# Hybrid decoder trunk on one core: attention units with their own step orders, weight splits moved within them, K weights scaled one pair ahead on GpSimd

## The chip, the cores and the metric

One core of one Trainium2 chip runs the whole program in one launch. The metric is the device time of that core in microseconds. The core has TensorE (PE for matmuls, PEld for its weight loads), VectorE (DVE), ScalarE (ACT), GpSimd (POOL) and SyncE (SP, which issues most DMAs here).

## The reference

Two layers over a residual stream of 1024 tokens by 1024 channels: a recurrent layer (RG-LRU) with a SwiGLU block, then a forgetting-attention layer with a SwiGLU block. The change lies in the attention layer:

```python
p = rmsnorm(h, norm_kv) @ w_kvf          # K, V and 16 forget logits
k, v, c = K heads, V heads, cumsum(log_sigmoid(f + b_forget))
q = rmsnorm(h, norm_mix[1]) @ w_q        # 16 heads of 64
for blk in range(8):                     # 128 queries each, causal
    s = q_blk @ k[:q1].T / 8 + c[q] - c[k]
    p = softmax(where(mask, s, -inf))
    out_blk = p @ v[:q1]
h = h + concat(out) @ w_o
```

All of it is float32 to the accuracy of a split: each matmul operand is written as high + low (both fp32r), and a product takes three matmuls.

## The kernel before, in words

Every engine has its own instruction stream, written out by hand and synchronised by counting semaphores; within an engine the order is fixed. Activations lie transposed in SBUF, 8 tiles of 128 channels by 1024 tokens (`xh`, `xl`). A weight piece of 128 x 1024 is loaded by SyncE into `raw`; ScalarE writes its high half `wh` (`split_hi`, L914), VectorE the low half `wl` (`split_lo`, L1256). `raw`, `wh` and `wl` have four slots; attention uses slots 0 and 1 in turn. In attention GpSimd first multiplies each `raw` piece by the norm's gain (`gain_piece`, L542).

Attention goes over 8 **pairs** of heads. Beside the scores of pair i, TensorE projects K and Q of pair i+1: 32 steps `p` of three 512-column matmuls each, eight for a half (1024 tokens are two halves of 512). After every eighth `p` VectorE must drain the one PSUM bank of the projections (`project_half`, L1588 for K, L1590 for Q) before the ninth may start. A pair has 8 **units** (2 heads x 4 ranges of 256 queries, ranges in the order 3, 0, 2, 1, so the unit's size differs). The steps of a unit are tokens of a string in `UNIT_STEPS`, and PE, ACT and DVE all walk through the same string:

- `S0`, `S1`: scores of the *next* unit, first and second 128 queries (L758 to L761). DVE takes the row maximum (`nmax`, L1667), ACT the exponential into `probs` (L1163).
- `T0`..`T3`: transposes of `probs` (L780), 256 keys each; ACT copies the high half `pth` (L1193), DVE the low half `ptl` (L1673). The first transpose of a unit waits for both exponentials.
- `V0`..`V3`: values times probabilities (L793), each waits for its `ptl`.
- `O`: the previous unit's output is added by ACT (`o_low`) and DVE into `resid`.
- `p`: a projection step (L746). `X`, `Y`: transposes of V (L823) and their two halves into `vs` (ACT L1183, DVE L1660 and L1661). `R`: the transposed row sums.

Ahead of unit 0 stands `A S0 S1 B` (called unit -1): `A` and `B` project V of this pair, 24 matmuls each. Between pairs ACT makes the halves of K (`kh`, L1130 and L1135) and of Q (L1147, L1148), DVE their low halves (L1596, L1602). `S1` of unit -1 shares its PSUM with `A` and waits until DVE has drained that (`kv_tmp`, L1655). `S1` of unit 0 uses the PSUM tile in which V was transposed, and waits until `vs` is written.

Pair 0 is written out, pairs 1 to 6 are a loop of three rounds of two, and pair 7 is written out without `p` steps. After it the output projection starts (`wo_tile`, L857) from `ohl`, the halves of the attention output (ACT L1152, DVE L1640), and its weight pieces, split by the same two routines.

Of the kernel before, what the change touches and what calls it, by code (L numbers as in the profile page):

```python
# [19 lines left out]
class Turns:  # L20
# [27 lines left out]


RANGE_ORDER = [3, 0, 2, 1]  # L50
UNIT_STEPS = {
# [4 lines left out]
}  # L56
PAIR_START = "A S0 S1 B"


WEIGHTS_AT = {(-1, "S1"): "K", (1, "S1"): "Q", (5, "S1"): "nextV"}  # L60


def pair_steps(with_p):

    steps = [(-1, s) for s in PAIR_START.split()]
    units = 2 * len(RANGE_ORDER)
    for u in range(units):
        for s in UNIT_STEPS[RANGE_ORDER[u % len(RANGE_ORDER)]].split():
            if u == 0 and s == "O" or u == units - 1 and s[0] == "S":
                continue  # L70
            steps.append((u, s))
            if (u, s) == (0, "T0"):
                steps += [(u, "X"), (u, "Y")]
            if (u, s) == (units - 1, "T1"):
                steps.append((u, "R"))
    steps.append((units, "O"))
    return [x for x in steps if x[1] != "p" or with_p]


def hawk_fox_yoco(nc, x, norm_mix, norm_ffn, w_ffn_in, w_ffn_out, w_rec_in, conv_w, conv_b,  # L80
# [11 lines left out]
    S, D = x.shape[1], x.shape[2]  # L92
# [7 lines left out]
    PAIRS = HEADS * HD // P  # L100
# [12 lines left out]
    pieces = Turns(4)  # L113
# [27 lines left out]
    STAT = {"start": 0, "recE": 1, "ffn0E": 2, "attE": 3, "ffn1E": 4}  # L141
    LRU_STEPS, FORGET_STEPS = 16, 10
    T_PAIR = RANGES * (RANGES + 1)

    with ExitStack() as life:
        def sb(name, shape, dt, at=life):
# [88 lines left out]
        v_filled = sem("v_filled")  # L235
# [35 lines left out]
        w_gained = sem("w_gained")  # L271
# [57 lines left out]
        GAIN = {"K": V_KV, "V": V_KV, "Q": V_MIX + KT}  # L329
# [184 lines left out]
        @block.gpsimd  # L514
        def _(pool):
            pool.memset(ident[:, :], 0.0)
            pool.memset(ones[:, :], 1.0)
            pool.memset(identb[:, :], 0.0)
            pool.memset(maskb[:, :], 0.0)
            pool.memset(negsel[:, :], 0.0).then_inc(const_zero, 1)  # L520
            pool.wait_ge(const_zero, 1)
            for m in (ident, identb):
                pool.affine_select(out=m[:, :], in_=m[:, :], compare_op=ALU.not_equal, fill=1.0, base=0,
                                   pattern=[[-1, P]], channel_multiplier=1)
            pool.affine_select(out=maskb[:, :], in_=maskb[:, :], compare_op=ALU.is_ge, fill=NEG, base=0,
                               pattern=[[-1, P]], channel_multiplier=1)
            pool.affine_select(out=negsel[:, :], in_=negsel[:, :], compare_op=ALU.not_equal, fill=-1.0, base=0,
                               pattern=[[-1, HEADS]], channel_multiplier=1).then_inc(const_zero, 1)
            pool.wait_ge(const_zero, 2)
            for n, base in enumerate((-32, -64, -96)):  # L530
                last = pool.affine_select(out=negsel[:, :], in_=negsel[:, :], compare_op=ALU.not_equal, fill=-1.0,
                                          base=base, pattern=[[-1, HEADS]], channel_multiplier=1)
                last.then_inc(const_ready if n == 2 else const_zero, 1)
                pool.wait_ge(const_ready if n == 2 else const_zero, 1 if n == 2 else 3 + n)

            def gain_piece(use, gain, n=P):

                slot, count = use
                pool.wait_ge(loaded[slot], count * 16)
                w = raw[slot][:, :].rearrange("p (k n) -> p k n", k=KT)[:, :, 0:n]  # L540
                g = vec[:, gain:gain + KT].unsqueeze(2).broadcast_to([P, KT, n])
                pool.tensor_tensor(w, w, g, ALU.mult).then_inc(w_gained, 1)  # L542

            def select(i):
                for j in range(2):
                    other = slice((1 - j) * HD, (2 - j) * HD)
                    pool.tensor_copy(q2[other, j, :], negsel[other, bass.ds(i * 2 + j, 1)].broadcast_to([HD, S])
                                     ).then_inc(sel_ready, 1)
                    pool.wait_ge(sel_ready, i * 2 + (j + 1))

            def scale_o(i):

                pool.wait_ge(rinv_loaded, i * 32 + 32)
                pool.wait_ge(o_added, i * UNITS + UNITS)
                o = resid[:, i, :] if isinstance(i, int) else resid[:, bass.ds(i, 1), :]
                r = rinv[:, :] if isinstance(i, int) else rinv[:, :].unsqueeze(1)
                pool.tensor_tensor(o, o, r, ALU.mult).then_inc(o_scaled, 1)

            def pool_pair(i, uses, with_p=True):
                pool.wait_ge(ql_ready, i * 2 + 2)  # L560
                if with_p:
                    gain_piece(uses["K"], GAIN["K"])
                    gain_piece(uses["Q"], GAIN["Q"])
                if not (isinstance(i, int) and i == 0):
                    scale_o(i - 1)
                if with_p:
                    pool.wait_ge(o_added, i * UNITS + 4)
                    gain_piece(uses["nextV"], GAIN["V"])
                    pool.wait_ge(s_filled, i * (2 * QB) + 2 * QB)
                    pool.wait_ge(w_gained, GAINED["V"](i + 1))  # L570
                    select(i + 1)

            gain_piece(pieces.use("forget", 0), V_KV, HEADS)
            for j, kind in enumerate("KQV"):
                gain_piece(pieces.use("attA", j), GAIN[kind])
            pool.wait_ge(c_ready, 1)
            pool.wait_ge(w_gained, GAINED["V"](0))
            select(0)
            pool_pair(0, att_uses(0))
            with pool.Fori(0, (PAIRS - 2) // 2) as it:  # L580
                for d in range(2):
                    pool_pair(it * 2 + (d + 1), att_uses(None, it, d))
            pool_pair(PAIRS - 1, att_uses(PAIRS - 1, None, 1), with_p=False)
            scale_o(PAIRS - 1)

# [316 lines left out]
        def _(act):  # L902
# [272 lines left out]
            def pair(i, uses, with_p=True):  # L1175
                high_q(i, f_before(i))
                for u, step in pair_steps(False):
                    m = int(step[1]) if len(step) > 1 else 0
# [15 lines left out]
                    elif step == "O":  # L1194
# [1 line left out]
                        if u >= 3:  # L1196
                            act.wait_ge(o_added, i * UNITS + (u - 2))
                        act.activation(o_low[(u - 1) % 2][:, :], o_ps[HD:P, :], ACT.Copy).then_inc(o_low_ready, 1)
                    if with_p and (u, step) in WEIGHTS_AT:
                        kind = WEIGHTS_AT[u, step]  # L1200
                        split_hi(uses[kind], att_free(kind, i),
                                 scaled=GAINED[kind[-1]](i + 1))
                    if with_p and (u, step) == (UNITS - 1, "T1"):
                        high_k(i + 1, f_before(i + 1) - 2)
                    if (u, step) == (UNITS - 1, "R"):
# [13 lines left out]
                for d in range(2):  # L1219
                    pair(it * 2 + (d + 1), att_uses(None, it, d))  # L1220
            pair(PAIRS - 1, att_uses(PAIRS - 1, None, 1), with_p=False)
            for m in range(2):
                split_hi(pieces.use("attE", m), (v_filled, 2 * PAIRS))
            act.wait_ge(o_added, PAIRS * UNITS)
            for k in range(PAIRS // 2, PAIRS):
                high_o(k)
# [22 lines left out]
        def _(dve):  # L1249
# [168 lines left out]
            steps = [2]  # L1418
# [224 lines left out]
            def pair(i, uses, with_p=True):  # L1643
# [3 lines left out]
                p = 0  # L1647
                for u, step in pair_steps(with_p):
                    m = int(step[1]) if len(step) > 1 else 0
# [43 lines left out]
                    elif step == "p":  # L1693
                        p += 1
                        if p % KT == 0:
                            q = p // KT - 1
                            project_half(q // 2, q % 2, kq_count(i + 1, q // 2, q % 2))
                    if with_p and (u, step) in WEIGHTS_AT:
                        split_lo(uses[WEIGHTS_AT[u, step]])

            pair(0, att_uses(0))
            with dve.Fori(0, (PAIRS - 2) // 2) as it:
# [52 lines left out]
```

## Time and profile before

| | |
|---|---|
| median of 3 runs | 2624.01 us (2622.91 to 2625.97) |
| the profiled execution | 2628.85 us, of which the span is 2627.0 us |
| PE busy | 2487.4 us (95%) |
| PEld, DVE, ACT, POOL busy | 77%, 48%, 30%, 3% |
| mean granted TensorE clock | 0.977 |
| attention pairs | from 1172.9 to 1744.8 us of the span |

TensorE is busy nearly all the time, so the places that count are the few in which it waits. The trace gives for every instruction its start and length and, where an engine sat idle before it, for how long and what ended that. A matmul's end is modelled: matmuls overlap, the next may start before the last one's end. Start to start is the safer measure.

### The profile page before, as it was taken

How to read it: one execution, taken by the hardware profiler on the slowest of the kernel's cores; microseconds unless marked ns; L12 is line 12 of the kernel's file. 1: busy time of each engine (PE TensorE's matmuls, PEld its weight loads, DVE VectorE, ACT ScalarE, POOL GpSimd, SP SyncE). 2: the span in 40 equal slices, each digit the busy share in tenths (PEclk: the TensorE clock that was granted, in tenths of full speed). 3: DMA queues.
4: the chain of work that ended last, by engine and by line, in shares of the span. 5: the costliest groups of instructions: out<-in, count | busy, mean ns of one | idle time of the engine just before them, and what ended most of it. 6: DMA issues, size and time to landing. Idle time of an engine off the chain costs nothing.

```text
span 2627.0 us, 28888 instructions
## 1 busy us (share of the span) xinstructions
PE 2487.4 (95%) x11449; PEld 2026.3 (77%) x11449; DVE 1262.3 (48%) x1257; ACT 782.6 (30%) x1045; POOL 85.9 (3%) x65
## 2 busy tenths in 40 slices
PE   7999889999999999989998989969999999999998
PEld 5888768888888888767777777757788888888887
DVE  6567664444444444465555555553444444444443
ACT  4443541111111111245454545542211111111112
POOL 0000000000000000010111111000000000000000
PEclk9999999999999999999999999989999999999998
DMA  3111011111111111111010110021111111111101
GB/s 113 57 56 48 24 33 55 50 48 48 48 48 48 48 48 49 56 48 33 25 33 24 32 30 26 25 89 48 48 49 49 49 49 51 50 48 48 48 24 64
DMA packets 164159, 122.65 MB, mean 47 GB/s; under 512 B 5136, under 2 KB 144640, under 8 KB 164096
## 3 DMA queue, kind: packets, MB, share of 16 engines
q1 hardware_dynamic: 162352, 117.52, 14.7%
q10 hardware_dynamic: 1744, 4.32, 0.6%
q8 instruction: 36, 0.59, 0.1%
q14 instruction: 27, 0.22, 0.0%
HBM read 113.37 MB, written 8.45 MB: 46 GB/s over the span
## 4 chain that ended last, share of the span: by engine, by line
PE 84%; DVE 6%; issue 5%; ACT 4%; DMA 1%; ACTq 0%; DVEq 0%; SPq 0%
PE ps L602 66%; PE ps L746 6%; PE ps L857 3%; PE ps L640 2%; PE ps L793 2%; PE ps L780 1%; DVE ptl L1673 1%; ACT pth L1193 1%; DVE nmax L1667 1%; PE ps L758 1%; PE ps L761 1%; PE ps L636 1%; ACT kh L1130 1%; ACT probs L1163 1%; ACT wh L914 0%
## 5 line engine op out<-in xcount | busy, mean ns | idle before, releaser
L602 PE MATMUL ps<-xh,wh 128*128 128x512 f32 x1680 | 519.5, 390 | 3.9 <-DVE wl L1256 2.5
L602 PE MATMUL ps<-xl,wh 128*128 128x512 f32 x1680 | 518.0, 390 | 0.0
L602 PE MATMUL ps<-xh,wl 128*128 128x512 f32 x1680 | 517.9, 389 | 0.0
L602 PEld LDWEIGHTS ps<-xh,wh 128*128 128x128 f32 x1680 | 315.9, 188 | 72.4 <-issue 7.0
L1293 DVE TENSOR_TENSOR tmp<-ps,rstd 128x1024 f32<-128x1024 f32 x96 | 117.3, 1224 | 528.0 <-PE ps L602 527.9
L602 PEld LDWEIGHTS ps<-xl,wh 128*128 128x128 f32 x1680 | 315.9, 188 | 65.8
L602 PEld LDWEIGHTS ps<-xh,wl 128*128 128x128 f32 x1680 | 315.8, 188 | 65.7
L1299 DVE TENSOR_TENSOR resid<-ps,resid 128x1024 f32<-128x1024 f32 x216 | 261.6, 1222 | 211.1 <-PE ps L602 211.1
L1256 DVE TENSOR_TENSOR wl<-raw,wh 128x1024 fp32r<-128x1024 f32 x193 | 236.9, 1232 | 218.4 <-ACT wh L914 218.3
L914 ACT ACTIVATE wh<-raw 128x1024 fp32r<-128x1024 f32 x193 | 201.3, 1049 | 417.8 <-PE ps L602 349.7
L602 PE MATMUL ps<-hh,wh 128*128 128x512 f32 x704 | 221.7, 396 | 9.8 <-DVE hl L1525 9.8
L602 PE MATMUL ps<-hl,wh 128*128 128x512 f32 x704 | 218.7, 392 | 0.0
L602 PE MATMUL ps<-hh,wl 128*128 128x512 f32 x704 | 218.3, 391 | 0.0
L1072 ACT ACTIVATE hh<-tmp 128x1024 fp32r<-128x1024 f32 x44 | 46.7, 1061 | 493.0 <-DVE tmp L1521 493.0
L746 PE MATMUL ps<-xh,wh 128*128 128x512 f32 x384 | 162.8, 424 | 16.6 <-DVE kv_tmp L1588 6.0
L602 PEld LDWEIGHTS ps<-hh,wh 128*128 128x128 f32 x704 | 132.9, 190 | 40.0 <-DVE hl L1525 10.7
L602 PEld LDWEIGHTS ps<-hl,wh 128*128 128x128 f32 x704 | 133.3, 189 | 28.2
L602 PEld LDWEIGHTS ps<-hh,wl 128*128 128x128 f32 x704 | 133.3, 189 | 28.2
L746 PE MATMUL ps<-xh,wl 128*128 128x512 f32 x384 | 153.4, 400 | 0.0
L746 PE MATMUL ps<-xl,wh 128*128 128x512 f32 x384 | 153.0, 398 | 0.0
L1068 ACT ACTIVATE tmp<-tmp 128x1024 f32<-128x1024 f32 x44 | 46.6, 1060 | 332.2 <-DVE tmp L1293 332.2
L1673 DVE TENSOR_TENSOR ptl<-ps,pth 128x512 fp32r<-128x512 f32 (+1 forms) x160 | 98.0, 634 | 88.2 <-ACT pth L1193 86.9
(184 smaller groups left out, 2796.1 us busy)
## 6 DMA issues: line engine op xcount, KB each, us to landing
raw<-in_w_ffn_in SPq DMA_DIRECT2D x88, 512.0 KB, 3.8
raw<-in_w_ffn_out SPq DMA_DIRECT2D x44, 512.0 KB, 3.3
raw<-in_w_rec_in SPq DMA_DIRECT2D x16, 512.0 KB, 5.2
raw<-in_w_kvf SPq DMA_DIRECT2D x16, 512.0 KB, 3.9
xin<-in_x SPq DMA_DIRECT2D x8, 512.0 KB, 6.9
raw<-in_w_rec_out SPq DMA_DIRECT2D x8, 512.0 KB, 4.0
raw<-in_w_q SPq DMA_DIRECT2D x8, 512.0 KB, 3.9
spill<-resid SPq DMA_DIRECT2D x8, 512.0 KB, 2.6
```

Source lines behind the costliest of these rows:

```text
L602: last = pe.matmul(acc[:, h], w, v[:, h], start=(k == 0 and p == 0), stop=(k == len(terms) - 1 and p == 2))
L640: last = pe.matmul(ps[3][:, h], ones[:, :], sq(seg, k)[:, h], start=(k == 0), stop=(k == KT - 1))
L746: last = pe.matmul(acc, w, v[:, k, h], start=(k == 0 and p == 0), stop=(k == KT - 1 and p == 2))
L793: last = pe.matmul(o_ps[:, q0 * P:2 * P], v, pt[t % 2][:, col:col + n], start=(kb == 0 and pt is pth), stop=(kb == 2 * r + 1 and pt is ptl))
L857: last = pe.matmul(acc[:, h], w, ohl[:, k, v, h], start=(k == 0 and p == 0), stop=(k == KT - 1 and p == 2))
L914: act.activation(wh[slot][:, :], raw[slot][:, :], ACT.Copy).then_inc(hi_ready[slot], 1)
L1068: act.activation(tmp[t][:, :], tmp[t][:, :], ACT.Silu).then_inc(silu_ready, 1)
L1072: act.activation(hh[:, t, :], tmp[2 + t][:, :], ACT.Copy).then_inc(hh_ready, 1)
L1256: dve.tensor_tensor(wl[slot][:, :], raw[slot][:, :], wh[slot][:, :].bitcast(F32), ALU.subtract).then_inc(lo_ready[slot], 1)
L1293: dve.tensor_tensor(dst, ps[slot][:, :], rstd[:, :], ALU.mult).then_inc(drained[slot], 1)
L1299: dve.tensor_tensor(resid[:, m, :], ps[slot][:, :], resid[:, m, :], ALU.add).then_inc(drained[slot], 1)
L1673: dve.tensor_tensor(ptl[t % 2][:, 0:width], t_ps[t % 2][:, 0:width], pth[t % 2][:, 0:width].bitcast(F32), ALU.subtract).then_inc(ptl_ready, 1)
```

## The change

Each of the 8 units now has its own string; `X`, `Y` and `R` stand in the strings, and the scores `S0`, `S1` of units 0, 2, 4 and 6 are spread between later steps. ACT's high split and DVE's low split of a weight piece now have places of their own (`HI_AT`, `LO_AT`). In pair 7 the first two output-weight pieces are split inside the pair (`OUT_AT`) and no longer behind it. GpSimd multiplies K of pair i+2 by its gain at the end of its work for pair i (`next_k`) where it did K of pair i+1 at the start; its loop is one round shorter for that, with the last round written out.

```diff
-UNIT_STEPS = {
-    3: "O T0 T1 S0 S1 p V0 T2 p V1 T3 p V2 p V3 p",
-    0: "O T0 S0 S1 p V0 p p",
-    2: "O T0 T1 S0 S1 p V0 T2 p V1 p V2 p",
-    1: "O T0 T1 S0 S1 p V0 p V1 p p",
-}
+UNIT_STEPS = [
+    "T0 X Y T1 p p p V0 T2 p V1 T3 S0 p V2 S1 V3",
+    "O T0 S0 S1 p V0 p p",
+    "O T0 T1 S0 p V0 T2 S1 p V1 p V2 p",
+    "O T0 T1 S0 S1 p V0 p V1 p p",
+    "O T0 T1 p p V0 T2 p V1 T3 S0 p V2 S1 p V3",
+    "O T0 S0 S1 p V0 p p",
+    "O T0 T1 S0 p V0 T2 S1 p V1 p V2 p",
+    "O T0 T1 R p p V0 p V1 p",
+]
...
-WEIGHTS_AT = {(-1, "S1"): "K", (1, "S1"): "Q", (5, "S1"): "nextV"}
+HI_AT = {(-1, "A"): "K", (1, "T0"): "Q", (5, "T0"): "nextV"}
+LO_AT = {(-1, "S1"): "K", (1, "V0"): "Q", (5, "V0"): "nextV"}
...
+    OUT_AT = {(1, "V0"): 0, (5, "V0"): 1}
...
-            def pool_pair(i, uses, with_p=True):
+            def pool_pair(i, uses, next_k=None, with_p=True):
                 pool.wait_ge(ql_ready, i * 2 + 2)
                 if with_p:
-                    gain_piece(uses["K"], GAIN["K"])
                     gain_piece(uses["Q"], GAIN["Q"])
...
                     gain_piece(uses["nextV"], GAIN["V"])
+                    if next_k is not None:
+                        gain_piece(next_k, GAIN["K"])
                     pool.wait_ge(s_filled, i * (2 * QB) + 2 * QB)
...
                         split_hi(uses[kind], att_free(kind, i),
                                  scaled=GAINED[kind[-1]](i + 1))
+                    if not with_p and (u, step) in OUT_AT:
+                        split_hi(pieces.use("attE", OUT_AT[u, step]), (v_filled, 2 * PAIRS))
...
             pair(PAIRS - 1, att_uses(PAIRS - 1, None, 1), with_p=False)
-            for m in range(2):
-                split_hi(pieces.use("attE", m), (v_filled, 2 * PAIRS))
             act.wait_ge(o_added, PAIRS * UNITS)
...
-            for m in range(2):
-                split_lo(pieces.use("attE", m))
```

In the order of TensorE's instructions, unit 0 of the first pair read so before, from its `T0` on (`kv_tmp` is V, `q2`, `qs`, `kl`, `kh` are the scores' operands, the last three rows a step `p`):

```order
L780 MATMUL ps2<-ident,probs0 128x128 x4
L823 MATMUL ps1<-ident,kv_tmp 128x128 x8
L780 MATMUL ps2<-ident,probs0 128x128 x4
L758 MATMUL ps0<-kl,q2 128x128
L760 MATMUL ps0<-maskb,identb 128x128
L761 MATMUL ps0<-kh,qs 128x128
L758 MATMUL ps1<-kl,q2 128x256
L760 MATMUL ps1<-maskb,identb 128x128
L761 MATMUL ps1<-kh,qs 128x256
L746 MATMUL ps3<-xh,wh1 128x512
L746 MATMUL ps3<-xl,wh1 128x512
L746 MATMUL ps3<-xh,wl1 128x512
```

Now, from the same `T0` (all lines of the program stand 5 lower from here on):

```order
L785 MATMUL ps2<-ident,probs0 128x128 x4
L828 MATMUL ps1<-ident,kv_tmp 128x128 x8
L785 MATMUL ps2<-ident,probs0 128x128 x4
L751 MATMUL ps3<-xh,wh1 128x512
L751 MATMUL ps3<-xl,wh1 128x512
L751 MATMUL ps3<-xh,wl1 128x512
L751 MATMUL ps3<-xh,wh1 128x512
L751 MATMUL ps3<-xl,wh1 128x512
L751 MATMUL ps3<-xh,wl1 128x512
L751 MATMUL ps3<-xh,wh1 128x512
L751 MATMUL ps3<-xl,wh1 128x512
L751 MATMUL ps3<-xh,wl1 128x512
```

The six matmuls of `S0` and `S1` are gone from behind `T1`, and three steps `p` stand there. The scores now come at the unit's end. Before, the last steps up to the next unit's `T0` (`probs1`) were:

```order
L746 MATMUL ps3<-xh,wh1 128x512
L746 MATMUL ps3<-xl,wh1 128x512
L746 MATMUL ps3<-xh,wl1 128x512
L793 MATMUL ps3<-pth1,vs 128x256
L793 MATMUL ps3<-ptl1,vs 128x256
L793 MATMUL ps3<-pth1,vs 128x128
L793 MATMUL ps3<-ptl1,vs 128x128
L746 MATMUL ps3<-xh,wh1 128x512
L746 MATMUL ps3<-xl,wh1 128x512
L746 MATMUL ps3<-xh,wl1 128x512
L780 MATMUL ps2<-ident,probs1 128x128 x3
```

Now, from `V2` on, they are:

```order
L798 MATMUL ps3<-pth0,vs 128x256
L798 MATMUL ps3<-ptl0,vs 128x256
L798 MATMUL ps3<-pth0,vs 128x256
L798 MATMUL ps3<-ptl0,vs 128x256
L763 MATMUL ps1<-kl,q2 128x256
L765 MATMUL ps1<-maskb,identb 128x128
L766 MATMUL ps1<-kh,qs 128x256
L798 MATMUL ps3<-pth1,vs 128x256
L798 MATMUL ps3<-ptl1,vs 128x256
L798 MATMUL ps3<-pth1,vs 128x128
L798 MATMUL ps3<-ptl1,vs 128x128
L785 MATMUL ps2<-ident,probs1 128x128 x3
```

`S1` (into `ps1`) now ends only four short matmuls ahead of the `T0` that needs its exponential, and no `p` stands between. On ScalarE, from unit 1's `O` to unit 2's `T0` and `T1`, stood before:

```order
L1198 ACTIVATE o_low<-ps 64x256
L1193 ACTIVATE pth<-ps 128x384
L1163 ACTIVATE probs,rsum<-ps,nmax 128x640
L1163 ACTIVATE probs,rsum<-ps,nmax 128x768
L914 ACTIVATE wh<-raw 128x1024
L1198 ACTIVATE o_low<-ps 64x256
L1193 ACTIVATE pth<-ps 128x512 x2
```

and now:

```order
L1203 ACTIVATE o_low<-ps 64x256
L1198 ACTIVATE pth<-ps 128x384
L919 ACTIVATE wh<-raw 128x1024
L1168 ACTIVATE probs,rsum<-ps,nmax 128x640
L1168 ACTIVATE probs,rsum<-ps,nmax 128x768
L1203 ACTIVATE o_low<-ps 64x256
L1198 ACTIVATE pth<-ps 128x512 x2
```

The split of Q's weights (`wh`) moves from behind the two exponentials to ahead of them. On VectorE the low split stays between the two maxima and the drain of K.

## Rows read from the trace of the kernel before

**Rows 1.** Stretches: us, busy us (instructions) of PE, PEld, DVE, ACT, POOL; granted clock; DMA.

```profile
1244.00:1315.80 71.80, 66.10 (x371) 53.75 (x370) 41.30 (x60) 38.16 (x74) 10.08 (x6) 0.98 0.11 30
1315.80:1386.20 70.40, 64.49 (x371) 52.35 (x370) 41.19 (x60) 38.17 (x74) 10.09 (x6) 1.00 0.11 31
1683.90:1744.80 60.90, 46.92 (x271) 38.91 (x270) 35.22 (x54) 31.99 (x67) 2.38 (x1) 0.91 0.03 9
...
1262.90:1266.30 3.40, 3.40 (x14) 3.11 (x14) 0.75 (x3) 1.02 (x4) 0.00 (x0) 0.50 0.02 7
```

**Rows 2.** TensorE's waits, pair 2: who waits for whom, us, times, longest.

```profile
PE ps L758 <- DVE vs L1661: 1.8, 1, 1.8
PE ps L793 <- DVE ptl L1673: 1.6, 4, 0.5
PE ps L758 <- DVE kv_tmp L1655: 0.9, 1, 0.9
PE ps L746 <- DVE kv_tmp L1588: 0.6, 1, 0.6
PE ps L746 <- DVE q_tmp L1590: 0.6, 1, 0.6
```

**Rows 3.** Timeline of unit 0, pair 2: start, length, engine, line, [idle before].

```profile
1329.83 0.60 PE L780 MATMUL ps<-ident,probs 128*128 128x128 f32 x4
...
1331.10 0.69 DVE L1673 TENSOR_TENSOR ptl<-ps,pth 128x512 fp32r<-128x512 f32 x1 [0.30 <-ACT pth L1193]
...
1333.70 0.68 DVE L1661 TENSOR_TENSOR vs<-ps,vs 128x512 fp32r<-128x512 f32 x1
...
1334.44 0.38 PE L758 MATMUL ps<-kl,q 128*128 128x256 f32 x1 [1.81 <-DVE vs L1661]
...
1334.90 0.63 DVE L1667 TENSOR_REDUCE nmax<-ps 128x1 f32<-128x128 f32 x2
...
1335.58 0.47 ACT L1163 ACTIVATE probs<-ps,nmax 128x256 f32<-128x256 f32 x1
...
1339.86 0.28 PE L793 MATMUL ps<-pth,vs 128*128 128x256 f32 x1
...
1340.26 0.45 PE L746 MATMUL ps<-xh,wh 128*128 128x512 f32 x1
...
1341.01 0.49 PE L780 MATMUL ps<-ident,probs 128*128 128x128 f32 x3
```

**Rows 4.** Timeline, units 1 and 2 of pair 2.

```profile
1343.46 0.80 ACT L1163 ACTIVATE probs<-ps,nmax 128x640 f32<-128x640 f32 x1 [1.36 <-DVE nmax L1667]
...
1345.22 1.05 ACT L914 ACTIVATE wh<-raw 128x1024 fp32r<-128x1024 f32 x1
...
1346.30 1.23 DVE L1256 TENSOR_TENSOR wl<-raw,wh 128x1024 fp32r<-128x1024 f32 x1 [2.01 <-ACT wh L914]
...
1348.18 0.50 PE L746 MATMUL ps<-xh,wh 128*128 128x512 f32 x1 [0.61 <-DVE kv_tmp L1588]
```

**Rows 5.** Timeline from pair 1's last unit to pair 2's second scores.

```profile
1310.59 0.93 PE L780 MATMUL ps<-ident,probs 128*128 128x128 f32 x7
...
1312.17 2.12 ACT L1130 ACTIVATE kh<-kv_tmp 64x1024 fp32r<-64x1024 f32 x2
...
1323.20 0.50 PE L758 MATMUL ps<-kl,q 128*128 128x512 f32 x1 [0.88 <-DVE kv_tmp L1655]
```

**Rows 6.** Timeline of GpSimd and VectorE at the start of pair 2.

```profile
1326.27 2.40 POOL L557 TENSOR_TENSOR resid<-resid,rinv 128x1024 f32 x1
...
1328.01 1.75 DVE L1256 TENSOR_TENSOR wl<-raw,wh 128x1024 fp32r<-128x1024 f32 x1 [2.22 <-ACT wh L914]
```

**Rows 7.** Timeline between the last pair and the output projection.

```profile
1750.12 6.79 DVE L1640 TENSOR_TENSOR ohl<-resid,ohl 128x1024 fp32r<-128x1024 f32 x4
...
1756.84 2.35 DVE L1256 TENSOR_TENSOR wl<-raw,wh 128x1024 fp32r<-128x1024 f32 x2
...
1758.16 2.05 PE L857 MATMUL ps<-ohl,wh 128*128 128x512 f32 x4 [12.43 <-DVE wl L1256]
```

More of the change, by code:

```diff
@@ L50 @@
 RANGE_ORDER = [3, 0, 2, 1]
-UNIT_STEPS = {
[4 rows of a table removed]
-}
+UNIT_STEPS = [
[8 rows of a table added]
+]
 PAIR_START = "A S0 S1 B"
-WEIGHTS_AT = {(-1, "S1"): "K", (1, "S1"): "Q", (5, "S1"): "nextV"}
+HI_AT = {(-1, "A"): "K", (1, "T0"): "Q", (5, "T0"): "nextV"}
+LO_AT = {(-1, "S1"): "K", (1, "V0"): "Q", (5, "V0"): "nextV"}
 def pair_steps(with_p):
     steps = [(-1, s) for s in PAIR_START.split()]
[L66 to L76, printed above, removed]
+    for u, unit in enumerate(UNIT_STEPS):
+        steps += [(u, s) for s in unit.split()]
+    steps.append((len(UNIT_STEPS), "O"))
     return [x for x in steps if x[1] != "p" or with_p]
@@ L568, in pool_pair @@
                     gain_piece(uses["nextV"], GAIN["V"])
+                    if next_k is not None:
+                        gain_piece(next_k, GAIN["K"])
                     pool.wait_ge(s_filled, i * (2 * QB) + 2 * QB)
-                    pool.wait_ge(w_gained, GAINED["V"](i + 1))
+                    pool.wait_ge(w_gained, GAINED["V"](i + 1) + (next_k is not None))
                     select(i + 1)
@@ L578, in _ @@
             select(0)
-            pool_pair(0, att_uses(0))
-            with pool.Fori(0, (PAIRS - 2) // 2) as it:
+            gain_piece(att_uses(0)["K"], GAIN["K"])
+            pool.wait_ge(w_gained, GAINED["K"](1))
+            pool_pair(0, att_uses(0), att_uses(None, 0, 0)["K"])
+            with pool.Fori(0, (PAIRS - 2) // 2 - 1) as it:
                 for d in range(2):
-                    pool_pair(it * 2 + (d + 1), att_uses(None, it, d))
+                    nxt = att_uses(None, it, 1) if d == 0 else att_uses(None, it + 1, 0)
+                    pool_pair(it * 2 + (d + 1), att_uses(None, it, d), nxt["K"])
+            last = (PAIRS - 2) // 2 - 1
+            pool_pair(PAIRS - 3, att_uses(None, last, 0), att_uses(None, last, 1)["K"])
+            pool_pair(PAIRS - 2, att_uses(None, last, 1))
             pool_pair(PAIRS - 1, att_uses(PAIRS - 1, None, 1), with_p=False)
@@ L1198, in pair @@
                         act.activation(o_low[(u - 1) % 2][:, :], o_ps[HD:P, :], ACT.Copy).then_inc(o_low_ready, 1)
-                    if with_p and (u, step) in WEIGHTS_AT:
-                        kind = WEIGHTS_AT[u, step]
+                    if with_p and (u, step) in HI_AT:
+                        kind = HI_AT[u, step]
                         split_hi(uses[kind], att_free(kind, i),
                                  scaled=GAINED[kind[-1]](i + 1))
+                    if not with_p and (u, step) in OUT_AT:
+                        split_hi(pieces.use("attE", OUT_AT[u, step]), (v_filled, 2 * PAIRS))
                     if with_p and (u, step) == (UNITS - 1, "T1"):
@@ L1697, in pair @@
                             project_half(q // 2, q % 2, kq_count(i + 1, q // 2, q % 2))
-                    if with_p and (u, step) in WEIGHTS_AT:
-                        split_lo(uses[WEIGHTS_AT[u, step]])
+                    if with_p and (u, step) in LO_AT:
+                        split_lo(uses[LO_AT[u, step]])
+                    if not with_p and (u, step) in OUT_AT:
+                        split_lo(pieces.use("attE", OUT_AT[u, step]))
             pair(0, att_uses(0))
```

## The prediction

> **What bounds the kernel now.** I read the views in this order. The page's sums say that TensorE is busy for 95% of the span, so only its waits count, and the change touches only attention. The view by stretches gives the pairs: pair 2 takes 70.4 us at full clock, pair 1 takes 71.8 us with one dip to half clock (1.2 of 2.4 GHz) of 3.4 us, and the last pair, which has no projections, 60.9 us [rows 1]. The view of waits, narrowed to pair 2, lists what TensorE stands for: 1.8 us until V's halves are written, 1.6 us in four waits for `ptl`, 0.9 us until VectorE has drained `A`, twice 0.6 us until it has drained a projection's half [rows 2]. Another 0.4 us goes before `X`, and those six sums are the whole idle time of the pair (70.40 - 64.49 = 5.9 us [rows 1]). A listed wait is shorter than what it costs: a `p` of three matmuls takes 0.75 us from start to start, 0.25 each, while one matmul lasts 0.45 in its row [rows 3], so each modelled end lies 0.2 us late. A wait costs its row and 0.2 us more.
>
> **The change, part by part.** The strings of the units only reorder: each pair has the same 32 `p`, the same scores, transposes and values. So I take away the waits that get cover and add those that lose it.
>
> Unit 0. From its `T0` to unit 1's `T0` go 11.18 us (1329.83 to 1341.01) [rows 3], the largest wait among them: `S1` stands until `vs` is written at 1334.38. Now three `p` of 0.7 to 0.8 us stand there, 2.2 us after `T1`, and what follows, `V0`, needs the same `vs`: it comes about 0.1 us after the third `p`. That takes away 1.8 + 0.2 - 0.1 = 1.9 us. But the exponential of `S1` now decides when unit 1's `T0` may start. Before, `S1` began at 1334.44; its maximum was out at 1335.53, the exponential ran from 1335.58 for 0.47, and some 0.1 us is left for reading out the row sum: 1.7 us in all. `S1` itself holds TensorE for 0.46 us, and `V3` for 0.40 (1339.86 to 1340.26) [rows 3]. So `T0` waits 1.7 - 0.46 - 0.40 = 0.8 to 0.9 us. Unit 0 nets 1.0 us. Before, five steps lay between and hid it.
>
> Units 1 and 5. ScalarE stands idle for 1.36 us ahead of its exponentials for unit 2, and the split of Q's weights, 1.05 us, came behind them at 1345.22; VectorE waited 2.01 us for it, its low split ran until 1347.53, and only then was K's half drained, which TensorE waited for until 1348.18 [rows 4]. With the high split behind `T0`'s `pth`, it fits into the 1.36 us with 0.3 to spare. The low split can start when the second maximum is out, about 0.9 us before 1345.22 (the second exponential runs in between), ends near 1345.5, and the drain waits for the eighth `p` alone. `O` and `ptl`, queued behind the drain, come earlier by about 1.2 us too. If that cover were gone, the split would delay both exponentials, and with them unit 2's `T0`, by at most 1.05 us per split. Units 5 and 6 repeat this with the next V's weights.
>
> Units 2 and 6. The two drain waits (0.6 each) and three of the four `ptl` waits (1.2 of the 1.6 us; the fourth is in unit 7) lie here [rows 2]. From a `T` to its `V` go 2.0 us (1329.83 until 1331.79 and the semaphore) [rows 3]. In the new string `V2` stands behind `T2` by `S1`, `p`, `V1`, `p`, some 2.7 us; ScalarE has one exponential of 0.6 us to do in between, which just fits. So all five go: 1.2 + 1.2 + 5 x 0.2 = 3.4 us.
>
> Unit 4. `S0` and `S1` move as in unit 0, but one `p` stands between `V3` and `T0`: 1.7 - 0.46 - 0.40 - 0.7 leaves 0.1 to 0.2 us of a new wait. Nothing was lost here before.
>
> Unit 7. One `p` more stands ahead of `V0`, which hides the fourth `ptl` wait (0.4 + 0.2). I count it at nothing. Behind this unit runs a chain that does not care for TensorE: ScalarE's four K halves start at 1312.17, right after `pth` of the `T0` of 1310.59, of which the first two take 2.12 us; then the other two, `o_low`, VectorE's add, its four low halves and the drain of `A`, until `S1` of unit -1 starts at 1323.20 [rows 5]. That is 12.6 us from `T0`; TensorE, freed, just waits there 0.6 us longer than now (0.88 listed).
>
> GpSimd. K's gain leaves the start of the pair and comes behind V's in unit 4. At the start it is not on the path: K's first `p` stands 10 us later. Here the row shows contention: the low split of K takes 1.75 us at 1328.01 while GpSimd's scaling runs until 1328.67 [rows 6], and 1.23 us alone [rows 4]. With GpSimd done 1.9 us earlier and the split moved up to about 1326, either finds its place before `B` ends at 1330. In unit 4 VectorE does only `ptl`, maxima and `o_low` additions, each with one operand in PSUM. The Trainium skill, page "SBUF — State Buffer", section "Who interferes with whom", says that a VectorE instruction with two SBUF inputs contends with a GpSimd instruction that reads SBUF, and one with at most one SBUF input doesn't; by that rule the moved gain costs nothing in unit 4, and the 1.75 us agree. `select`, queued behind it, has until the next pair. SyncE's loads are released by the same low splits, in the same order, K's some 2 us earlier: nothing.
>
> So a pair nets 1.9 - 0.9 + 3.4 - 0.2 = 4.2 us, and seven pairs 29 us. The waits at the loop's back edge (between pairs 2 and 3, and 4 and 5) are untouched.
>
> The clock. Pairs 1, 4, 5 and 6 each have a dip of 3.4 us that begins at the `vs` wait, such as the one at 1262.9; it costs 71.8 - 70.4 = 1.4 us [rows 1]. Pair 2 has the same wait and no dip. The new order still has 1.5, 0.4 and 0.9 us of waiting within some 20 us. I take half of the four dips away: 3 us; ends 0 and 6. The Trainium skill, "TensorE: Matmul & The Clock Gate", section "What's actually happening", says that the default is the throttled state and that activity releases it. By that alone all four dips would go, and the sum would be 3 us lower; the rows of pair 2 show that the wait is not enough to cause one.
>
> Pair 7 has no `p` to cover anything. Unit 0 gains 0.9 us (the `vs` wait, less what it puts before `V3` and `T0`). In units 2 and 6 `V0` comes sooner in the string, while ScalarE and VectorE must do the output weights' halves (1.05 and 1.23 us [rows 4]) ahead of `o_low` and `pth`: `V0` 0.7 us later, and `S1`'s exponential, now behind `T2`'s `ptl`, 1 us later: 1.7 us each. Unit 4 loses 0.7. Sum +3 us; ends 0 and 6.
>
> The end. Behind pair 7 TensorE waits 12.43 us for the first output weight's low half, which VectorE makes only after four low halves of `ohl` (from 1750.12 for 6.79 us, 1.7 each) [rows 7]. With the weights ready, the first matmuls can start after the first of the four, near 1751.9, but are then fed at 1.7 and later 1.2 us per tile of six matmuls, which take 1.36 at full clock; seven tiles are fed until 1759.4, and the other nine follow: 1759.4 + 10 x 1.36 = 1773, against 1781.6 before. The first tiles run at half clock, 2.7 us each; I take 6 us of the 8.4 (ends 4 and 8.5).
>
> The sum: -29 - 3 + 3 - 6 = -35 us. The profiled execution took 2628.85 us (span 2627.0), which gives 2594; against the median of 2624.0, 4.8 us lower, 2589.
>
> **The rivals.** First, late scores: `S0`, `S1` behind `T3` put their maxima and exponentials into the queues just before `T0`'s `pth`; if each such join in units 0, 2, 4 and 6 costs 0.7 us more than worked out, a pair nets 1.5 us, and the time is 2624 - 10 - 6 = 2608. For it speaks that the exponential in unit 2 fits only just; against it the 2.0 us from `T` to `V`, which hold. Second, more than forecast: all dips vanish (3 us more), the end gives 8.5, pair 7 loses nothing: 2624 - 29 - 6 - 8.5 = 2580, and with a start chain that gives back unit 7's 0.6 per pair, 2576. Third, on the other side, the clock: the waits now gather at the pair's start and at unit 1's `T0`. If TensorE fell to 1.2 GHz there for long, at 1.4 us lost per 3.4 us of dip, then 40 us, that is 97 us of dips or 14 us in each pair, make it slower: 2630 and above. Pair 2 with 5.9 us of idle time and no dip speaks against it. Fourth, the covers bring nothing, as the chain of ScalarE and VectorE through a whole pair decides, and only pair 7 and the end count: 2624 + 3 - 6 = 2621. Against it: they are busy for 38 and 41 of 70 us [rows 1].
>
> **How the numbers follow.** As worked out, 2589 (its own range 2579 to 2600): 0.60. More: 0.08. Late scores, 2600 to 2618: 0.20. No change, within 0.2% (5.2 us, about what a measurement of this kernel can tell): 0.05. Slower: 0.07. The range of 2573 to 2607 leaves out the last two, some 0.06 of the late scores and 0.01 below. Faster 0.88, same 0.05, slower 0.07.
>
> **What would show it.** In the profile after: the wait on `vs` gone from `S1` and under 0.3 us at `V0`; no wait of a `p` on L1588 or L1590's drain; one wait of 0.8 us at unit 1's `T0` on `probs`; the wait of unit -1's `S1` near 1.5 us; pairs of 66 us; the first output matmul some 6 us after the last value. It would be wrong if pairs stay above 69 us, if `T0` waits over 2 us, or if the granted clock in attention falls below the 0.98 of pair 1.

## The result and the profile after

The changed kernel takes **2587.64 us** (median of 4 runs, 2585.63 to 2593.28), the kernel before, run beside it, 2624.28 us. The ratio is 0.9864, with a 95% interval of 0.9846 to 0.9881. Its profiled execution took 2588.48 us. The page of the profile after:

```profile
span 2586.7 us, 28872 instructions
PE 2471.5 (96%) x11449; PEld 2021.3 (78%) x11449; DVE 1266.3 (49%) x1257; ACT 787.3 (30%) x1045; POOL 85.9 (3%) x65
```

The same stretches as in [rows 1], in the kernel after: pairs 1, 2, 3 and 7.

```profile
1236.90:1302.90 66.00, 63.38 (x371) 52.62 (x370) 41.87 (x60) 38.61 (x74) 10.09 (x6) 1.00 0.11 33
1302.90:1369.20 66.30, 63.50 (x371) 52.70 (x370) 42.25 (x60) 38.74 (x74) 10.07 (x6) 1.00 0.12 33
1369.20:1441.60 72.40, 66.69 (x371) 54.66 (x370) 40.83 (x60) 38.75 (x74) 10.05 (x6) 0.95 0.10 30
1645.50:1710.00 64.50, 46.10 (x271) 38.39 (x270) 37.41 (x56) 35.02 (x70) 2.38 (x1) 0.92 0.03 9
```

Pair 2 has gone from 70.4 to 66.3 us, the last pair from 60.9 to 64.5. Pair 1, which had a dip to half clock before, has none now. In pair 2, TensorE's list of waits, against [rows 2]:

```profile
PE ps L763 <- DVE kv_tmp L1660: 1.5, 1, 1.5
PE ps L785 <- ACT probs L1168: 0.7, 1, 0.7
PE ps L828 <- DVE kv_tmp L1660: 0.4, 1, 0.4
PE ps L798 <- DVE vs L1666: 0.2, 1, 0.2
```

Together 2.8 us, which is 66.30 - 63.50, the pair's whole idle time; it was 5.9 us. The two waits for a projection's drain and the four for `ptl` are gone. The wait for `vs` has shrunk to 0.2 us and stands at `V0`, the one ahead of `S1` of unit -1 has grown from 0.9 to 1.5 us, and one of 0.7 us at unit 1's `T0` is new. This is unit 0 on the timeline after, against [rows 3]:

```profile
1322.34 0.38 PE L798 MATMUL ps<-pth,vs 128*128 128x256 f32 x1 [0.17 <-DVE vs L1666]
...
1326.32 0.28 PE L763 MATMUL ps<-kl,q 128*128 128x256 f32 x1
...
1326.88 0.42 DVE L1672 TENSOR_REDUCE nmax<-ps 128x1 f32<-128x256 f32 x1 [0.48 <-PE ps L766]
...
1327.34 0.47 ACT L1168 ACTIVATE probs<-ps,nmax 128x256 f32<-128x256 f32 x1 [0.45 <-DVE nmax L1672]
...
1327.96 0.55 PE L785 MATMUL ps<-ident,probs 128*128 128x128 f32 x3 [0.71 <-ACT probs L1168]
```

`S1` begins at 1326.32 and unit 1's `T0` at 1327.96: 1.64 us, in which maximum and exponential run one behind the other with nothing beside them on TensorE but `V3`. Next, units 1 and 2 after, against [rows 4]:

```profile
1329.01 1.05 ACT L919 ACTIVATE wh<-raw 128x1024 fp32r<-128x1024 f32 x1
...
1330.47 0.80 ACT L1168 ACTIVATE probs<-ps,nmax 128x640 f32<-128x640 f32 x1 [0.41 <-DVE nmax L1672]
...
1331.22 1.22 DVE L1261 TENSOR_TENSOR wl<-raw,wh 128x1024 fp32r<-128x1024 f32 x1
...
1332.68 0.69 DVE L1593 TENSOR_TENSOR kv_tmp<-ps,rstd 128x512 f32<-128x512 f32 x1 [0.25 <-PE ps L751]
```

ScalarE's idle time ahead of the exponential is 0.41 instead of 1.36 us, with the high split in it. VectorE goes into the low split without a wait, where it stood for 2.01 us, and the drain (`kv_tmp`, last row) now waits for TensorE and not TensorE for it. At the end, against [rows 7]:

```profile
1715.76 11.35 DVE L1645 TENSOR_TENSOR ohl<-resid,ohl 128x1024 fp32r<-128x1024 f32 x8
...
1717.14 2.05 PE L862 MATMUL ps<-ohl,wh 128*128 128x512 f32 x4 [6.58 <-DVE ohl L1645]
...
1720.36 1.59 PE L862 MATMUL ps<-ohl,wh 128*128 128x512 f32 x4 [0.32 <-DVE ohl L1645]
```

TensorE waits 6.58 us for the first `ohl` low half where it waited 12.43 us for the weights.

The balance of the two profiled executions, from the trace (start to start): pairs 0 to 6 took 511.0 us before and 473.4 now (-37.6), pair 7 +3.6, from the last value's first matmul to the 96th of the output 36.5 and 31.1 us (-5.4), what lies ahead of pair 0 -0.9. Together -40.3, the difference of the spans. The last of these is chance: over all traces pair 0 starts between 1170.5 and 1174.9 us.

### The profile page after: what moved, and what is told of

Read it like the earlier page. It is cut to its first block, busy times and chain, and to the rows that moved or that the text cites. A ratio compares the mean times of both kernels' runs of the same rounds, so it can differ in the third digit from the quotient of the medians.

```text
span 2586.7 us, 28872 instructions
## 1 busy us (share of the span) xinstructions
PE 2471.5 (96%) x11449; PEld 2021.3 (78%) x11449; DVE 1266.3 (49%) x1257; ACT 787.3 (30%) x1045; POOL 85.9 (3%) x65
## 4 chain that ended last, share of the span: by engine, by line
PE 90%; DVE 4%; issue 3%; ACT 2%; DMA 0%; ACTq 0%; SPq 0%; DVEq 0%
PE ps L607 67%; PE ps L751 8%; PE ps L862 3%; PE ps L798 3%; PE ps L785 2%; PE ps L645 2%; PE ps L766 1%; PE ps L763 1%; PE ps L641 1%; ACT kh L1135 1%; DVE kl L1601 0%; DVE kv_tmp L1660 0%; DMA xin<-in_x 0%; PE ps L828 0%; DVE wl L1261 0%
## 5 line engine op out<-in xcount | busy, mean ns | idle before, releaser
L607 PEld LDWEIGHTS ps<-xl,wh 128*128 128x128 f32 x1680 | 315.6, 188 | 65.7
```

What stands on the lines that cost most here:

```text
L607: last = pe.matmul(acc[:, h], w, v[:, h], start=(k == 0 and p == 0), stop=(k == len(terms) - 1 and p == 2))
```

## The experiments

All times are medians of 4 to 10 runs (but for the last kernel, one run) beside runs of the kernel before on the same chip (2624.2 to 2625.9 us). "Pair" is the length of pair 2, or of pairs 4 and 6 where pair 2 has a dip of the clock.

**The strings alone.** Splits (those of the output weights too) and gain go back to their old places; the cut shows the two tables.

```diff
-HI_AT = {(-1, "A"): "K", (1, "T0"): "Q", (5, "T0"): "nextV"}
-LO_AT = {(-1, "S1"): "K", (1, "V0"): "Q", (5, "V0"): "nextV"}
+HI_AT = {(-1, "S1"): "K", (1, "S1"): "Q", (5, "S1"): "nextV"}
+LO_AT = {(-1, "S1"): "K", (1, "S1"): "Q", (5, "S1"): "nextV"}
...
```

> The new step strings alone: weight splits at S1 of units -1, 1 and 5 as before, K's gain at the pair's start as before, the output weights' splits behind pair 7. If the strings and the splits each carry a part (my theory): unit 0 keeps its 1.1 us, units 2 and 6 still meet a late drain of the projection bank, since the split lies ahead of it, and keep only about 0.5 us each; a regular pair takes 68.5 us, the dips at unit 0 stay away, the first output matmul waits 12 us again; about 2606 us. Rival, the strings do all: pairs of 66.3 us, 2592 us. Rival, the splits do all: pairs of 70.4 us, 2624 us.

Measured: 2618.58 us, ratio 0.9979 [0.997, 0.9989], pair 69.7 us. That is 0.7 us per pair, much less than expected. TensorE's waits in its pair 2:

```profile
PE ps L748 <- DVE kv_tmp L1590: 1.2, 1, 1.2
PE ps L748 <- DVE q_tmp L1592: 1.2, 1, 1.2
PE ps L782 <- ACT probs L1165: 0.7, 1, 0.7
```

The drain waits have doubled, 0.6 to 1.2 us each. With the late split, the drain comes at a time that VectorE sets, and the new string of unit 2 has the `p` that needs it one step `S1` earlier. What the strings save at `ptl` they mostly give back at the drain: from `T0` to the next unit's `T0`, units 2 and 6 take 8.14 and 8.36 us, only 0.2 us less each than before.

**The old strings, the rest of the change.** All eight units go back to them; the cut shows the string of units 2 and 6:

```diff
-    "O T0 T1 S0 p V0 T2 S1 p V1 p V2 p",
+    "O T0 T1 S0 S1 p V0 T2 p V1 p V2 p",
...
```

> The old step strings with all the rest of the change (early high splits, K's gain one pair ahead, output weights split inside pair 7). My theory: the drain waits of units 2 and 6 go and the V0 waits with them, V2 still waits about 0.5 us, unit 0 keeps its 1.8 us wait and its dips to half clock; a regular pair takes 67.4 us, the end gives 5.5 us; about 2600 us. Rival, only the strings matter: pairs of 70.4 us, about 2618 us with the end's gain.

Measured: 2594.08 us, ratio 0.989 [0.9874, 0.9907], pair 67.0 us: 3.4 us less than before. Its waits in pair 2:

```profile
PE ps L763 <- DVE vs L1666: 1.8, 1, 1.8
PE ps L763 <- DVE kv_tmp L1660: 0.9, 1, 0.9
PE ps L828 <- DVE kv_tmp L1660: 0.4, 1, 0.4
PE ps L798 <- DVE ptl L1678: 0.4, 1, 0.4
```

Both drain waits and three of the four `ptl` waits are gone without the new strings. The two runs add up: 0.7 + 3.4 = 4.1 us, the whole gain of the pair. The splits' places are the larger part.

**Scores of unit 0 early**, the other strings as changed:

```diff
-    "T0 X Y T1 p p p V0 T2 p V1 T3 S0 p V2 S1 V3",
+    "T0 X Y T1 S0 S1 p V0 T2 p V1 T3 p V2 p V3 p",
```

> The changed kernel with only unit 0's string as before (S0 S1 behind T1, the wait for vs in front of S1). My theory: each pair 1.1 us longer (the 1.8 us wait for vs back, the 0.7 us wait for the exponential gone), 8 us in all, and dips to half clock at unit 0 return in three to five pairs at 1.6 us each: 2601 us. Rival, the dips hang on total idle time of the pair and not on this wait: no dips, 2596 us.

Measured: 2598.54 us, 0.9893 [0.9872, 0.9915], pair 67.0 us (pairs 4 and 6; pair 2 took 68.7 with a dip in unit 0). The new string of unit 0 is worth 0.7 us, not the 1.1 expected. Seven times that is 5 of the 10.9 us by which this kernel is slower than the changed one; in its trace the rest is mainly the dip in pair 2 and one in pair 0, some 1.6 us each, and pair 7, 2.7 us longer at a mean clock of 0.82. Together with the runs above, 0.7 us is all that the strings bring to a pair: once the split is early, the new ones save 0.2 us in each of units 2 and 6 (6.72 and 6.82 us with the old strings, 6.50 and 6.61 with the new), and unit 4 gives that back.

**K not ahead.** K's gain returns to the start of GpSimd's work for the pair, its high split to behind `S1`.

```diff
-HI_AT = {(-1, "A"): "K", (1, "T0"): "Q", (5, "T0"): "nextV"}
+HI_AT = {(-1, "S1"): "K", (1, "T0"): "Q", (5, "T0"): "nextV"}
...
+                    gain_piece(uses["K"], GAIN["K"])
                     gain_piece(uses["Q"], GAIN["Q"])
...
-                    if next_k is not None:
-                        gain_piece(next_k, GAIN["K"])
```

> The changed kernel with K multiplied by its gain at the pair's start and its high split behind the second exponential, as before. My theory: no pair changes by more than 0.1 us, 2588 us; K's low split takes 1.7 us again at the start of a pair. Rival, the gain ahead frees VectorE on the path of B's drain: X waits longer, pairs 0.5 us or more longer, 2592 us.

Measured: 2589.08 us, 0.9868 [0.9851, 0.9884], pair 66.3 us, no different from the changed kernel. Its low split of K took 1.76 us again, as in [rows 6].

**Output splits behind the last pair**, as before the change (VectorE's low halves likewise):

```diff
-                    if not with_p and (u, step) in OUT_AT:
-                        split_hi(pieces.use("attE", OUT_AT[u, step]), (v_filled, 2 * PAIRS))
...
+            for m in range(2):
+                split_hi(pieces.use("attE", m), (v_filled, 2 * PAIRS))
             act.wait_ge(o_added, PAIRS * UNITS)
```

> The changed kernel with the first two output weights split behind pair 7 as before. My theory: the first output matmul waits some 12.5 us instead of 6.6, of which only 5.4 us show at the end of the first two tiles, and pair 7 is shorter by the splits that leave it, 2.5 to 3 us; together 2 to 3 us slower than the changed kernel, 2590 us. Rival, the splits cost pair 7 nothing: 5 to 6 us slower, 2593 us. Rival, the start of the first matmul decides alone: 2594 or more.

Measured: 2592.7 us, 0.9884 [0.9867, 0.99]. Pair 7 took 63.8 us (the changed kernel 64.5), and the first output matmul stood behind VectorE again:

```profile
1725.52 2.05 PE L862 MATMUL ps<-ohl,wh 128*128 128x512 f32 x4 [13.24 <-DVE wl L1261]
```

From the pair's end to the first output matmul it is 13.8 us, in the changed kernel 7.2. So the splits save 6.6 us behind the pair and seemed to cost 0.7 within it. The expectation (2590 us, with pair 7 shorter by 2.5 to 3) missed, and the time is that of its first rival, 2593: splits that cost the pair nothing. That they do cost it something is worked out below, under pair 7.

**The old strings in pair 7 alone**:

```diff
-                for u, step in pair_steps(with_p):
+                for u, step in pair_steps(with_p, not with_p):
...
```

> The changed kernel with the old strings in pair 7 alone, which has no projection steps. My theory: pair 7 goes from 64.5 to about 62 us (60.9 before; the two output splits inside it stay), 2585 us. Rival, pair 7's loss is all due to the splits: 64.5 us as now, 2588 us.

Measured: 2586.13 us, 0.9847 [0.9824, 0.9869], pair 7 64.5 us where 62 was expected, as if the strings cost nothing there.

**Output splits' high halves one step earlier**, at `T0` of units 1 and 5, the low halves left at `V0`:

```diff
+    OUT_HI_AT = {(1, "T0"): 0, (5, "T0"): 1}
...
-                    if not with_p and (u, step) in OUT_AT:
-                        split_hi(pieces.use("attE", OUT_AT[u, step]), (v_filled, 2 * PAIRS))
+                    if not with_p and (u, step) in OUT_HI_AT:
+                        split_hi(pieces.use("attE", OUT_HI_AT[u, step]), (v_filled, 2 * PAIRS))
```

> The changed kernel with the high splits of the two output weights in pair 7 moved from V0 to T0 of units 1 and 5, ahead of the exponentials, the low splits left. My theory: as in the regular pairs ScalarE has room there, unit 2 and 6 of pair 7 no longer wait for o_low and pth behind a split, pair 7 falls from 64.5 to 62.5 us at like clock, 2586 us. Rival, pair 7's length is set by its low clock: 64 to 66 us, no change, 2588 us.

Measured: 2586.66 us, 0.9853 [0.9838, 0.9868], pair 7 63.6 us (expected 62.5). The waits for `ptl` in pair 7, in the changed kernel and then in this one:

```profile
PE ps L798 <- DVE ptl L1678: 6.4, 6, 1.9
```

```profile
PE ps L799 <- DVE ptl L1679: 2.7, 3, 1.1
```

With the splits behind the pair they were 3.7 us, in a second trace of the changed kernel 5.3. So at these waits the splits' place costs 1.6 to 2.7 us, and the earlier high half takes it back.

**A shorter chain at the pair's start.** VectorE's fourth low half (`low_q(i, 1)`), which only the later scores need, goes behind the maximum of `S1` of unit -1:

```diff
-                for j in range(2):
-                    low_k(i, j)
-                    low_q(i, j)
+                low_k(i, 0)
+                low_q(i, 0)
+                low_k(i, 1)
...
+                        if (u, step) == (-1, "S1"):
+                            low_q(i, 1)
```

> The changed kernel with VectorE's low half of the second head's Q moved behind the second row maximum of the pair, out of the chain that ends in A's drain. My theory (that chain sets the start of S1 in unit -1): S1's wait falls from 1.5 us to about 0.4, every regular pair from 66.3 to 65.1 us, 2579 us. Rival, ScalarE's halves of K and Q set it: wait and pairs unchanged, 2588 us.

Measured: 2581.78 us, 0.983 [0.9808, 0.9851]. Its pair 2, and the first wait of the changed kernel's list there:

```profile
1301.90:1367.00 65.10, 63.54 (x371) 52.69 (x370) 40.92 (x60) 38.73 (x74) 10.57 (x6) 1.00 0.12 33
```

```profile
PE ps L763 <- DVE kv_tmp L1660: 0.2, 1, 0.2
```

The wait falls from 1.5 to 0.2 us: the chain of ScalarE and VectorE sets when this `S1` starts. The time stays above the expected 2579 us, as pair 7 took 65.9 us at a mean clock of 0.82 (64.5 at 0.92 in the changed kernel).

**Scores together**: `S1` of units 0 and 4 two steps earlier, so that `p` and `V2` stand behind it (the cut shows unit 0).

```diff
-... V1 T3 S0 p V2 S1 V3",
+... V1 T3 S0 S1 p V2 V3",
...
```

> The changed kernel with S0 and S1 of units 0 and 4 together behind T3, ahead of p and V2. My theory: S1 then starts 2.0 us ahead of the next unit's T0, its chain takes 1.7, so both waits on probs go and no ptl comes late: pairs of 65.4 us (0.7 at unit 1, 0.15 at unit 5), 2582 us. Rival, the maxima and exponentials push ptl of T2 or T3 back: V2 or V3 wait instead, pairs stay at 66.3 us, 2588 us.

Measured: 2586.27 us, 0.9851 [0.9829, 0.9873], pair 65.5 us, as expected; the wait at unit 1's `T0` is 0.2 instead of 0.7 us. Pair 7, at a mean clock of 0.82, took 66.7 us, which takes back some of the gain; 2582 us was expected.

**All of it together**: the short start chain, the scores together, the old strings in pair 7 and the early high output splits, the four edits above and no other.

> The changed kernel with four edits: the low half of the second head's Q behind the second maximum, S0 and S1 of units 0 and 4 together, the old strings in pair 7 alone, and the high splits of the two output weights in pair 7 behind T0 of units 1 and 5. If the savings found one by one add up (my theory): regular pairs of 66.3 - 1.2 - 0.8 = 64.3 us, pair 7 shorter by 1 to 3 us, about 2572 us. Rival, unit 1's wait and the start chain share their cause, so that only the larger counts: pairs of 65.1 us, 2578 us.

Measured: **2568.57 us**, 0.978 [0.9766, 0.9793]. It beats both kernels, the changed one by 21 us (2589.61 us beside it). The pairs are as expected, and pair 7, at 60.7 us, is back at its length of before with the output weights ready. Its pairs 2 and 3, and its waits in pair 2:

```profile
1300.30:1364.60 64.30, 63.31 (x370) 52.62 (x369) 40.73 (x60) 38.52 (x74) 10.58 (x6) 1.00 0.12 34
1364.60:1433.00 68.40, 64.91 (x370) 53.39 (x369) 40.82 (x60) 38.47 (x74) 10.98 (x6) 0.98 0.11 31
```

```profile
PE ps L841 <- DVE kv_tmp L1673: 0.4, 1, 0.4
PE ps L776 <- DVE kv_tmp L1673: 0.2, 1, 0.2
PE ps L811 <- DVE vs L1679: 0.2, 1, 0.2
PE ps L798 <- ACT probs L1181: 0.2, 1, 0.2
```

One microsecond of waiting is left in the pair.

**Each kernel once more**, to see what varies between executions of the same code.

> The changed kernel once more, beside the others on one chip: 2588 us. If the dips to half clock at unit 0 hang on the waits, none in pairs 1 to 6 except behind the loop's back edge; if on chance, one to three. Pair 7 between 64 and 67 us by its clock.

> The kernel before once more, for its clock: if the dips at unit 0 belong to its order, three to five of pairs 1 to 6 have one and these pairs take 1.4 to 1.6 us more; if they are chance, none or one. 2624 us.

Measured: 2589.61 us, 0.9863 [0.9848, 0.9878], for the changed kernel; its pairs without a loop edge agree with the first trace within 0.1 us, pair 7 took 65.2 us. The kernel before, one run: 2621.76 us. Its pairs 1 to 3 agree within 0.1 us; pairs 4 and 6 took 70.4 instead of 72.0, since their dips are missing. Here is pair 4 in the first trace and then in the second:

```profile
1462.50:1534.60 72.10, 66.16 (x371) 53.73 (x371) 41.25 (x60) 38.35 (x74) 10.09 (x6) 0.98 0.11 29
```

```profile
1461.10:1531.60 70.50, 64.57 (x371) 52.37 (x370) 41.17 (x60) 38.21 (x74) 10.08 (x6) 1.00 0.11 30
```

## Why the prediction was right, and where its terms were off

**Unit 0** (forecast -1.0 us): from `T0` to `T0` 10.4 us instead of 11.18 (-0.8). The wait for `vs` is gone up to 0.17 us at `V0`, and `T0` waits 0.7 us for `S1`'s exponential, listed, 0.9 by the rule of 0.2 us. The run with early scores in unit 0 gives 0.7 us as well: right.

**Units 1, 2, 5 and 6** (forecast -3.4): the stretches from `T0` to the next unit's `T0` in units 2 and 6 went from 8.33 and 8.59 us to 6.50 and 6.61, 3.8 together. The size was right, but a step in it was not. My working credited the new strings with the `ptl` waits ("In the new string `V2` stands behind `T2` by `S1`, `p`, `V1`, `p`"). By the runs with the strings alone and the old strings, the early split does nearly all of it (8.33 and 8.59 to 6.72 and 6.82 us with the old strings, 3.4 of the 3.8): `ptl` is queued on VectorE behind the late drain, and comes in time when the drain does. Where two parts of a change each remove the same wait, only undoing one shows which of them did it.

**Unit 4** (forecast 0.1 to 0.2 lost): 7.64 to 8.03 us, 0.4 lost. Some 0.2 us of it stand ahead of the `p` behind `T1` (1.02 us from `T0` to it, 0.79 to the `S0` that stood there), which I had not counted; the forecast wait ahead of unit 5's `T0` is there with 0.2 us.

**Unit 7 and the start chain** (forecast 0): right. Unit 7 is 0.6 us shorter and the wait ahead of `S1` 0.6 longer. From unit 7's `T0` (1298.32) to that `S1` (1310.93) it is 12.6 us, the same as before. The run with the shorter chain confirms what sets it.

**GpSimd and K ahead** (forecast 0): right for the time. Two rows show how. At the pair's start the low split of K is now slower than in [rows 6], as it starts while GpSimd still works:

```profile
1312.60 2.39 POOL L555 TENSOR_TENSOR resid<-resid,rinv 128x1024 f32 x1
...
1313.43 2.64 DVE L1261 TENSOR_TENSOR wl<-raw,wh 128x1024 fp32r<-128x1024 f32 x1
```

It ends at 1316.07, 1.08 us after GpSimd is done at 1314.99, as if it had stood until then. It stays hidden: VectorE's next work, the drain of `B`, begins at 1317.83. In unit 4 the two products with `ptl` run beside the moved gain in the same 1.29 us as alone 13 us later:

```profile
1346.79 1.29 DVE L1678 TENSOR_TENSOR ptl<-ps,pth 128x512 fp32r<-128x512 f32 x2
1346.85 3.75 POOL L540 TENSOR_TENSOR raw<-raw,vec 128x1024 f32<-128x1024 f32 x2 [31.86 <-DVE resid L1690]
...
1359.37 1.29 DVE L1678 TENSOR_TENSOR ptl<-ps,pth 128x512 fp32r<-128x512 f32 x2
```

Both agree with what the Trainium skill says on the page "SBUF — State Buffer", section "Who interferes with whom": a VectorE instruction with two SBUF inputs contends with a GpSimd instruction that reads SBUF, one with a single SBUF input doesn't.

So a pair nets 4.1 us (forecast 4.2). That it comes so close is partly luck: units 2 and 6 gave 0.4 us more than forecast, units 0 and 4 together 0.4 less. The first rival, late scores, would have netted 1.5, and is out. So is the fourth, by which the covers bring nothing, and the third, by which the clock makes it slower: the mean granted clock of the profiled executions rose from 0.977 to 0.982.

**The clock** (forecast 3 us, half of four dips). All four dips at `vs` are gone, some 5.6 us by what pairs 1, 4, 5 and 6 were longer for them (1.4, 1.6, 1.0 and 1.6). One at the start of pair 0 is gone too, but by chance: it stands behind a wait of 2.0 us that all 14 traces have there, and five of them have the dip, two of these with the new strings. And the second trace of before has only one of the four at `vs` itself. Over all traces with the 1.8 us wait in unit 0 (before twice, old strings, unit 0 early), 7 of 24 of the pairs 1 to 6 have a dip in unit 0; over the ten in which it is covered, 0 of 60. The wait thus brings dips, by chance, and covering it removes them. (One of the 60 pairs, with the strings alone, has a dip elsewhere, behind the 1.2 us wait for Q's drain.) The term was sound in size for the typical run, and four dips were that trace's luck: its execution, 2628.85 us, lies above the range of the runs shown. That is also why the profiles differ by 40.3 us and the medians by 36.6. The other trace of each gives spans of 2619.9 and 2583.7, a difference of 36.2.

**Pair 7** (forecast +3): +3.6 in the first traces, +3.9 in the second. Its length hangs on how many dips fall into it, so the runs on its cause can be set side by side only with the granted clock. The same code of pair 7 took 64.5 us at 0.92 and 65.2 at 0.90 (changed); 62.7 at 0.93 and 64.5 at 0.89 (old strings everywhere, or there alone); 63.8 at 0.89 twice (splits behind). Taking away 0.41 us for each us at half clock (1.4 of 3.4), an estimate, leaves about 60 for the changed pair, 59 with old strings, 58 with the splits behind, 57 with neither (before) and 58 with the high splits early. That is too coarse to tell the parts: in the run "K not ahead" pair 7 has the changed kernel's code and took 65.7 us at 0.87, which leaves 59, and runs at a mean clock of 0.82, such as "scores together", don't fit the estimate at all.

The units, from `T0` to `T0`, tell more. Units 2 and 6 of pair 7 take 7.7 and 8.0 us in the changed kernel, 6.2 and 6.7 with the splits behind, 6.7 and 6.6 with the high splits early: the splits' place costs 1.0 to 1.5 us in unit 2 (the 7.7 and 6.7 hold 3.4 us at half clock, the 6.2 none) and 1.3 to 1.4 in unit 6. Before the change they took 6.2 each, so that the loss is 1.5 and 1.8 us, where 1.7 each was forecast. Unit 4, with the new string, went from 6.0 to 7.0 us, both at full clock (forecast 0.7 lost), and unit 0 from 10.1 to 9.5 (forecast 0.9 gained; in the second traces 9.7 to 9.5). The start of the pair is 0.6 us longer and unit 7 0.6 shorter, which I had not counted and which cancel. The mechanism held, and the exact length is chance: with a dip of 3.4 us in it, in the second trace, unit 4 took 8.0 us.

**The end** (forecast -6): -5.4. The first matmuls started 6.6 us after the last value. With the splits behind, pair 7 and this end took 101.6 us instead of 95.6, and the median was 5.1 us higher. The working had a slip: four low halves at 1.7 us and three at 1.2 end near 1760.5 and not 1759.4, which leaves 7.5 us to gain and not 8.4.

**The sum**: forecast -35, measured -36.6 between medians, inside the range given for "as worked out".

## What to carry to other kernels

A split or copy that no matmul needs soon can still hold back TensorE, when a drain is queued behind it on the same engine: look for the engine's own idle gap ahead of it, and move it there. Before crediting a wait to one part of a change, ask whether another removes it too, and whether the part alone exposes a step that was covered by what it moved. Where one execution's trace shows dips of the clock, take a second trace before pricing them: their count is chance, their cause is not.

## What the runs showed of the hardware that was not expected

The dips vary between executions of one program: four at the same wait in one trace of before, one in the next. The Trainium skill, page "TensorE: Matmul & The Clock Gate", section "What's actually happening", says that the throttled state is the default and that activity releases it. The traces agree in that the dips come at waits, and show that one and the same wait of 1.8 us has a dip behind it in 7 of 24 cases only. Length alone does not tell: the wait of 1.3 to 1.5 us ahead of `S1` of unit -1 had none behind it in 36 cases (pairs 1, 2, 4 and 6 of the nine traces that have it).

Pairs 3 and 5, behind the loop's back edge, are 4.1 to 6.4 us longer than a pair without edge or dip in every kernel (6.9 where a dip at `vs` comes on top). In pair 3 of the changed kernel ScalarE stands 3.94 us without a releaser, TensorE 2.66 us behind it, and the clock is at half for 6.8 us:

```profile
1374.82 1.06 ACT L1152 ACTIVATE qs<-q_tmp 64x1024 fp32r<-64x1024 f32 x1 [3.94 <-issue]
...
1377.47 0.49 PE L763 MATMUL ps<-kl,q 128*128 128x512 f32 x1 [2.66 <-DVE qs L1607]
```

Such a stand of ScalarE, 3.8 to 4.4 us, is there at both edges of all 14 traces. In each of these 28 cases one DMA transfer of the kind "instruction" (queue 14) starts 1.6 to 2.1 us before ScalarE goes on, here at 1373.06. That fits a wait for the loop's code, which no run tests.

With all of it together pairs 3 and 5 took 68.4 and 68.8 us instead of 72.4 and 71.3. A regular pair is 2.0 us shorter there too; the remaining 2.0 and 0.5 us go with a dip behind the edge of 3.4 us, not 6.8. With the short start chain alone pair 5 had the short dip as well, pair 3 had not. I had not expected that, and what makes it shorter was not tried.
